# Three transformer blocks on one Trainium2 core: loads of the first stage by need, and a new order and new tables in the route stage

## The reference, cut to what matters

```
def rmsnorm(x, g):
    x32 = x.astype(jnp.float32)
    y = x32 * lax.rsqrt(jnp.mean(x32 * x32, axis=-1, keepdims=True) + RMS_EPS)
    return (y * g.astype(jnp.float32)).astype(x.dtype)
...
    h = rmsnorm(x, norm_mix[0]);  qkv = h @ w_qkv            # first projection, 1024 x 1536
...
    y = _headnorm(_dir_merge(y), GN_EPS) * gn_w + gn_b       # per head, over 64 channels
    x = _layernorm(ALPHA * x + g1 * (mixed[:, CTX_LEN:] @ w_out[l]), ln1_g[l], ln1_b[l])
    ffn = _hier_moe(_modulate(x, sh2, sc2), ...)             # 4 groups x 8 experts, top 2 of one group
    x = _layernorm(ALPHA * x + g2 * ffn, ln2_g[l], ln2_b[l])
```

## Time and profile before

| | us |
|---|---|
| median of 3 runs | 3330.69 |
| the runs | 3324.12 to 3330.73 |
| the profiled execution | 3329.68 |
| its span | 3327.9 |
| TensorE busy in the span | 2990.6 (90%) |
| VectorE busy | 1954.2 (59%) |
| ScalarE busy | 1250.8 (38%) |
| GpSimd busy | 898.5 (27%) |

### The profile page before, as it was taken

How to read it: one execution, slowest core, us unless ns; L and a number is a source line. 1 busy time by engine, 2 the same in 40 slices (tenths; PEclk the granted TensorE clock), 3 DMA queues, 4 the chain that set the end, 5 groups by cost and what they waited for, 6 DMA issues and landing times. The chain is left out here.

```text
span 3327.9 us, 54357 instructions
## 1 busy us (share of the span) xinstructions
PE 2990.6 (90%) x22320; PEld 2383.9 (72%) x22320; DVE 1954.2 (59%) x2725; ACT 1250.8 (38%) x1572; POOL 898.5 (27%) x468
## 2 busy tenths in 40 slices
PE   7989999998999979999989999558999869999993
PEld 5567888797777757888768777247776458888882
DVE  3656562201433335654299837866573759999996
ACT  2544322222333333332132221502222147777773
POOL 3023344343222213444322210001010024444531
PEclk9989999999999999999989998778999979999997
DMA  3633222322111102222221100221112359999995
GB/s 144 229 126 114 90 100 97 130 96 76 64 64 51 64 26 102 100 101 89 101 77 64 51 31 1 109 106 29 42 41 84 106 204 356 366 373 368 378 364 221
DMA packets 82354, 443.90 MB, mean 133 GB/s; under 512 B 19312, under 2 KB 22384, under 8 KB 33392
## 3 DMA queue, kind: packets, MB, share of 16 engines
q1 hardware_dynamic: 72656, 431.59, 35.1%
q0 software_dynamic: 9504, 9.47, 0.8%
HBM read 426.31 MB, written 39.86 MB: 140 GB/s over the span
## 5 line engine op out<-in xcount | busy, mean ns | idle before, releaser
L77 POOL TENSOR_TENSOR ring_lo<-ring,unit_hi 128x2048 fp32r<-128x2048 f32 x116 | 534.4, 4607 | 1109.0 <-ACT unit_hi L72 1109.0
L130 PE MATMUL wide<-h_hi,unit_hi 128*128 128x512 f32 x1296 | 516.1, 398 | 44.9 <-DVE h_lo L191 23.0
L132 PE MATMUL wide<-h_hi,ring_lo 128*128 128x512 f32 x1296 | 508.1, 392 | 0.0
L131 PE MATMUL wide<-h_lo,unit_hi 128*128 128x512 f32 x1296 | 507.9, 392 | 0.0
L3183 DVE TENSOR_TENSOR ex_w_lo<-ring,ex_w_hi 128x2048 fp32r<-128x2048 f32 x192 | 437.7, 2289 | 41.0 <-ACT ex_w_hi L3133 39.8
L3133 ACT CAST ex_w_hi<-ring 128x2048 fp32r<-128x2048 f32 x192 | 365.6, 1908 | 107.3 <-DMA ring<-in_weights 94.5
L72 ACT CAST unit_hi<-ring 128x2048 fp32r<-128x2048 f32 x116 | 221.3, 1908 | 406.5 <-PE wide L132 404.9
L130 PEld LDWEIGHTS wide<-h_hi,unit_hi 128*128 128x128 f32 x1296 | 245.2, 189 | 110.6 <-POOL ring_lo L77 18.8
L132 PEld LDWEIGHTS wide<-h_hi,ring_lo 128*128 128x128 f32 x1296 | 245.3, 189 | 52.3
L131 PEld LDWEIGHTS wide<-h_lo,unit_hi 128*128 128x128 f32 x1296 | 245.7, 190 | 49.3 <-issue 0.2
L362 DVE TENSOR_TENSOR ffn_hidden_lo<-ffn_whole,ffn_hidden_hi 128x512 f32 (+1 forms) x44 | 200.4, 4554 | 51.8 <-ACT ffn_hidden_hi L337 51.8
(11 more groups left out here) (519 smaller groups left out, 5935.2 us busy)
## 6 DMA issues: line engine op xcount, KB each, us to landing
ring<-in_weights SPq DMA_DIRECT2D x356, 1024.0 KB, 5.9
factors<-rp_out SPq DMA_DIRECT2D x8, 1536.0 KB, 5.5
rw_F<-factors SPq DMA_DIRECT2D x12, 1024.0 KB, 5.9
tail_both<-pair_rows_out SPq DMA_DIRECT2D x4, 1024.0 KB, 8.3
x<-in_x SPq DMA_DIRECT2D x1, 2048.0 KB, 7.6
x_kept<-x SPq DMA_DIRECT2D x1, 2048.0 KB, 12.0
x<-x_kept SPq DMA_DIRECT2D x1, 2048.0 KB, 8.7
x_mixing<-x SPq DMA_DIRECT2D x1, 2048.0 KB, 8.4
```

The source lines that it names most:

```text
L77: pool.tensor_tensor(self.lo[n % RING][:, :], self.ring[n % RING][:, :], self.hi[n % 2][:, :].bitcast(F32), ALU.subtract).then_inc(self.lo ...
L130: pe.matmul(dst, a[0], b[0], start=start, stop=False)
L131: pe.matmul(dst, a[0], b[1], start=False, stop=False)
L132: return pe.matmul(dst, a[1], b[0], start=False, stop=stop)
```

## The change

In the first stage: unit 0 and the gains are loaded first; x follows in eight parts, each with a semaphore of its own, then unit 1, the identity, units 2 and 3. TensorE begins with 24 plain fp32 products of ones that nothing reads. VectorE, not GpSimd, makes `ring_lo` of units 0 and 1. ScalarE makes all `h_hi` first, then the `hi` of unit 1, then the squares; VectorE likewise. The product with the sum of squares moves from ahead of chunk 2 to ahead of chunk 3, the transposes of `rstd` from ahead of chunk 4 to ahead of chunk 5, and the columns are taken between copies.

In the route stage: the sums of squares stand ahead of all projection, and spreads and turns stand between pieces of projection. `member` gets an empty tile before and behind, so that four products with ones of 160 to 64 columns and one with the triangle give the counts and the total. The slot table is built in fp32r; its second half holds only the choice, is filled only by the second choice (products of 256 columns for n = 1, of 128 for n = 0), and VectorE makes 2 x token + choice of it.

In the expert stage: the three rows are loaded behind the last units, and `results` is filled with one row in place of 128.

```
+WARM_UP = 24
...
     def scalar(self, act, k):
+        if self.fresh:
+            act.wait_ge(self.c.x_loaded[k], 16)
         act.activation(self.h[0][:, k, :], ...)
-        if self.fresh:
-            self.sq.square(act, k)
...
         if self.fresh:
+            between(dve)
+            for k in range(DC):
+                self.sq.add(dve, k)
             self.mean(dve)
...
             def _(sp):
+                for k in range(DC):
+                    sp.dma_start(x[:, k, :], x_of[:, k, :]).then_inc(c.x_loaded[k], 16)
+                w.load(sp, 1)
+                sp.dma_start(c.ident[:, :], ident).then_inc(c.ident_loaded, 16)
+                for n in range(2, RING):
+                    w.load(sp, n)
...
             def _(pool):
-                for n in range(U_QKV_A):
+                for n in range(2, U_QKV_A):
                     w.write_lo(pool, 0, n)
...
             def _(pe):
+                for n in range(WARM_UP):
+                    pe.matmul(bank[7][:, 0:P], c.ones[:, :], c.ones[:, :], start=True, stop=True)
                 for m_ in range(DC + KVC):
                     if m_ % 2 == 0:
                         unit = w.parts(pe, 0, m_ // 2)
-                    if m_ == 2:
+                    if m_ == 3:
                         normed.tensor(pe)
-                    if m_ == 4:
+                    if m_ == 5:
+                        pe.wait_ge(c.ident_loaded, 16)
                         normed.turn(pe)
...
                 for k in range(DC):
                     normed.scalar(act, k)
-                    if k == 1:
-                        w.write_hi(act, 0, 1)
+                w.write_hi(act, 0, 1)
+                for k in range(DC):
+                    normed.sq.square(act, k)
                 normed.root(act)
...
             def _(dve):
-                normed.vector(dve)
+                w.write_lo(dve, 0, 0)
+                normed.vector(dve, lambda eng: w.write_lo(eng, 0, 1))
...
                 head.tensor_sums(pe)
+                head.tensor_squares(pe)
                 tile(0, (0, 1), 0, MC)
-                head.tensor_squares(pe)
-                tile(1, (0, 1), 0, MC)
                 head.tensor_spread(pe, 0)
                 head.tensor_spread(pe, 1)
...
+                ahead = member[:, :, :].rearrange("p t e -> p (t e)")
+                for s in range(TT):
+                    pe.matmul(counts[:, s * EXPERTS:], c.ones[:, :], ahead[:, 0:(TT + 1 - s) * EXPERTS], start=(s == 0), stop=False)
+                pe.matmul(counts, earlier[:, :], ahead[:, EXPERTS:], start=False, stop=True).then_inc(ranks_done, 1)
+                for n in (1, 0):
+                    pe.wait_ge(low_ready, 2 - n)
+                    pe.wait_ge(named_ready, 2 - n)
                     for t in range(TT):
-                        mm = pe.matmul(SLOTS_AT, at_low[:, n, t, :], named[:, n, t, :, :].rearrange("p v h -> p (v h)"),
-                                       start=(n == 0 and t == 0), stop=(n == 1 and t == TT - 1))
+                        mm = pe.matmul(SLOTS_AT[:, 0:(n + 1) * P], at_low[:, n, t, :], named[:, n, t, :, :].rearrange("p v h -> p (v h)")[:, 0:(n + 1) * P],
+                                       start=(n == 1 and t == 0), stop=(n == 0 and t == TT - 1))
...
-                for to, of in rows_of:
-                    sp.dma_start(to, of).then_inc(rows_loaded, 16)
                 with sp.Fori(0, rounds_of(sp)) as r:
...
                         sp.dma_start(w.ring[n % RING][:, :], w.stream[n]).then_inc(w.loaded[n % RING], 16)
+                for to, of in rows_of:
+                    sp.dma_start(to, of).then_inc(rows_loaded, 16)
...
-                    pool.dma_start(results[:, p, :], tokens[0:P, :]).then_inc(scattered[p], 16)
+                    pool.dma_start(results[0:1, p, :], tokens[0:1, :]).then_inc(scattered[p], 16)
```

More of the change, by code:

```diff
@@ L3499, in program @@
         w.lo = lo
-        inputs = nc.alloc_semaphore("inputs_loaded")
+        c.x_loaded = [nc.alloc_semaphore(f"x_loaded{k}") for k in range(DC)]
+        c.cols_loaded, c.ident_loaded = nc.alloc_semaphore("cols_loaded"), nc.alloc_semaphore("ident_loaded")
         with nc.Block() as block:
```

100 lines of the change are left out of this document (49 added, 51 removed).

## The result

| us | before | changed |
|---|---|---|
| median | 3328.49 | 3303.22 |
| the runs | 3324.12 to 3330.73 | 3296.45 to 3307.58 |
| ratio, 95% interval | | 0.9919 [0.9903, 0.9935] |
| the profiled execution, its span | 3329.68, 3327.9 | 3296.45, 3294.7 |

The change is 0.8% faster: 22 to 32 us by the interval, 33.2 by the two profiled executions. A second series of the changed kernel gave 3305.79 and the same ratio, 0.9919 [0.9905, 0.9932]. So two things need an answer: where the time went, and why the profiles show more than the medians do.

The account below looks back on a forecast made before the run. TensorE's products set the experts' pace; gains come only elsewhere. 3329.7 - (13.8 + 8.1 + 3.5 + 5.6 + 5.0 - 0.3 = 35.7) + 1.0 = 3295.0 us; own range 3289 to 3300, 3287 to 3307 with most rivals.

Parts of the forecast that it names:

- Start: First stage: first product at 11.6 us, chunk 4 at 37.1 instead of 51.44, later rstd transposes cost 0.5; gain 13.8 us.
- Head of the route stage: Squares put ahead of projection let VectorE's chain of norms start earlier: gain 8.1 us, bounds 6.7 to 8.7.
- so no new wait: Head of the route stage: TensorE's last tile still leads VectorE's need by 1.1 us, 2.5 before.
- Tables: Route stage: ranks in 10 records instead of 28 gain 3.5 us; slot table, 6.9 against 12.5, gains 5.6.
- Entry: Start of the experts: first gather no longer queued behind 2.5 MB, landing at 2692; gain 5.0 us, bounds 0 to 7.5.
- with 2 to 2.5 us to land: Experts' entry: the gather, its issue perhaps held to 2689.7 by VectorE's subtraction, lands after that time, at 2692.
- tail term of -0.3: End of the experts: row loads moved behind the last ring loads may touch the last scatter, a loss of 0.3 us.
- I let it slide along unchanged: Attention, feed-forward, mixer and some 560 us of experts depend on no absolute time, so they were taken as unchanged.
- (a): Rival, chance 0.14: products of ones are dear or x is late; start gains 3 to 8 us, say 3303.
- (b): Rival, chance 0.14: the experts are bound by their weight stream, so an earlier gather gives nothing; 3300 us.
- (c): Rival, chance 0.05: narrow fp32r products, or ranks of 160 columns, cost what the old ones did; 3301 us.
- (d): Rival, chance 0.03: less rest lowers the experts' granted clock, each per cent 5.6 us; at 10%, 3357 us.

Follow-up runs that it names:

- the parts alone: Four kernels, each the kernel before with one part of the change: first stage 0.9959, head of the route stage 0.9981, tables 0.9977, entry 0.9989.
- half the loads: The changed kernel with only the first half of each unit of expert weights loaded (results not those of the reference); its one execution took 3291.21 us.

## Why the prediction was right, and where not

The forecast was 3295.0 and the median is 3303.2: inside the range of 3287 to 3307, 3 us above the forecast's own range, and faster, as forecast. By its own steps:

- **Start, 13.8 forecast, 13.4 found.** First product 11.6 forecast, 10.57 found; sum of squares 28.2 and 27.04; from the sum to chunk 4, 8.9 and 8.91; a wait of 2.5 and 2.41. All of it is 1.1 earlier, since unit 0 landed at 5.5, not 6.65. What the forecast left out is the clock behind that wait: it set aside 0.4 us for the short pause ahead of the first product, which cost nothing (it was 0.4 to 1.5 us in seven profiles, and the first product took 0.47 in all), and nothing for the longer one, which cost 1.5 where the clock fell. At the start of chunk 4 the gain was 15.5, not 14.3, and then 2.1 were lost, not 0.5: that 13.4 stands so near to 13.8 is in part luck, two misses that cancel. The products of ones took 0.15 a record, below both bounds of the forecast, since the clock rose under them.
- **Head of the route stage, 8.1 forecast, 7.2 found.** Up to the first gate the steps hold: the squares' end 6.2 behind the sums forecast and 6.4 found, the gate 37.1 and 36.8, and TensorE kept its clock. The step that failed is "so no new wait": it counted TensorE's lead over VectorE only. The turns had moved in TensorE's list, and ScalarE's roots stood behind their copies all the time; the last copy came at 2584.90, 0.5 behind the moment at which VectorE wanted its root. It cost 1.4 us. The 8.1 and the 7.2 both stand on the profile of before, with its low clock in tile 0; by the four profiles with the old head the gain is 4.6 to 7.2, in the mean 6.1.
- **Tables, 3.5 and 5.6 forecast, 3.5 and 5.5 found.** The narrow products cost what their nearest rows said. By the mean of the profiles the second is 5.0.
- **Entry, 5.0 forecast, 2.9 found.** The step "with 2 to 2.5 us to land" is wrong: it took away the 2.5 MB that had been ahead of the gather and overlooked the ring's units, the first of which VectorE's subtractions free 0.8 us before the gather's issue ends. The forecast had seen VectorE hold the issue, not that it lets the ring's loads go. Its tail term of -0.3 is not to be seen: 50.4 and 50.3.
- **"I let it slide along unchanged"**: true of the code, not of its time. The 561 us of experts have a scatter of 12 us, by late weights and by the end of the last expert, and the profile of before, on which the sum stood, was the shortest of nine profiles in that stage (577.7 against a mean of 583.3 with the old entry).

In sum the four places give 32.5 us where 35.7 were forecast; that is 3.2 of the 8.2 by which the median is above the forecast. The rest is between the 32.5 and the 25 to 28 us that medians of 4 or 5 runs show, with an interval of 22 to 32; the parts alone give 31.4, and the means over all profiles 30.8. So some 2 of the 32.5 come from a profile of before that was slow at the changed places. Whether longer experts take some of the 3 to 6 us that are left stays open.

**The rivals.** (a) The products of ones were not dear and x not late: it was complete at 12.9, where the forecast wanted it at 13, and TensorE did not wait for it. Eight loads beat one by their early first part. (b) The experts are not bound by their stream, as half the loads show, but they stand near to it: the stage is 1 to 13 us longer than with half the loads, by late units and at the end of the last expert; it is a scatter, not shown to be an answer to the change. (c) The tables did what was meant. (d) No clock was lost in the steady part of the experts: 1.00 in the windows of both.

## What to carry to other kernels

When an operation is moved in one engine's list, look at who copies its result on another engine, and at what stands behind that copy in that engine's list; here this was the only new wait. A DMA that is on the path competes with those that other engines' progress sets free, so count what will be issued until it lands, not only what is queued ahead of it. And compare profiles stage by stage, and more than one of each kernel: a gain is read at the place of the edit, not from the span, where unchanged stages differed by up to 12 us. Even there the old code differed by 1.5 and 2.7 us from profile to profile, by its clock, and a single one of them overstated the gain.

## What was not expected of the hardware

- A gather's issue by GpSimd takes 1.10 us alone and 3.13 beside VectorE's subtraction of two operands in SBUF.
- Whether a wait of TensorE costs its clock differs from execution to execution. Waits of 0.4 to 1.5 us ahead of the first product left it up in seven profiles (0.47 us each), one of 3.94 did not (0.77). The wait of 2.4 us ahead of chunk 4 was followed by a fall in six profiles (at once or up to 1.4 us behind it; granted clock 0.50) and by none in one.
- Long work with short pauses, as in the mixer, differs with the same instructions: 480.9 to 481.4 us in some profiles and 483.3 to 486.0 in others, with granted clocks of 0.90 to 0.91 and of 0.89 to 0.90.
- Eight loads of 256 KB in flight together moved 308 GB/s between 5.5 and 10.5 us, one of 2 MB 397; but their first part was there 3.6 us before the whole.
